# Two transformer-like blocks on one core: half of a projection tile moves behind the fourth branch's turns, a gate tile runs whole, and a copy goes ahead of an eviction

## The chip, the core and the metric

The kernel runs on one core of one Trainium2 chip. The core's engines run beside each other and meet only at semaphores: TensorE (PE in the profile; PEld is its weight load), VectorE (DVE), ScalarE (ACT), GpSimd (POOL) and SyncE (SP), which here only issues DMA. TensorE writes its products to PSUM, which has eight banks. The metric is the device time of one execution in microseconds, the median of the runs shown.

## The reference

All data are fp32, for 256 tokens of width 1024. A first block (attention and a linear recurrence, then a mixture of 16 experts) is followed by two layers of a second block. The change touches these two layers only. Cut to what matters, a layer is:

```
h = rmsnorm(x, norm_g[l])
c = split_columns(h @ w_in[l])                 # 1024 x 3564
y_a = attention A * silu(gate)                 # four branches, 4 heads of 64 each
y_b = attention B * silu(gate)
y_c = (compressed + selected + window) * silu(gate)
y_d = stick_breaking_attention(q, k, v) * silu(gate)
for i, y in enumerate((y_a, y_b, y_c, y_d)):
    gate = sigmoid(h @ w_merge[l, i] + b_merge[l, i])
    merged = merged + gate * (y @ w_branch[l, i])
x = x + merged @ w_out[l]
```

Stick-breaking attention, the fourth branch, takes for each query `a = exp(log_sigmoid(z) + after)`, where `after` sums `log_sigmoid(-z)` over the keys behind, and returns `a @ v`.

## The kernel before

A weight matrix is cut into tiles of 512 rows by 512 columns. SyncE loads a tile, ScalarE makes its high part (`high`, L426) and VectorE the rest (`low`, L435), each in two halves; every product then takes three matmuls, high by high, high by low and low by high. ScalarE's split of a tile waits until the tile before it in the ring of buffers is used.

In a layer, tiles 0 to 13 are the input projection `w_in` (L559, two tiles for one block of columns, 24 matmuls of 512 columns each; tiles 12 and 13 are block 6), and G[0] to G[15] are the gate products `h @ w_merge` (L639, 48 matmuls of 256 columns each). A block of products takes two PSUM banks, even blocks banks 0 and 1, odd blocks banks 2 and 3. The first gate block (G[0] and G[1]) has the banks of block 6, so its first matmul waits until ScalarE has evicted block 6 (`evict(6)`, L2611).

The attention runs in twelve groups: the kinds A, D, B, cmp, slc and win, each for the first and the second 128 query rows. Groups 2 and 3 are the fourth branch, D0 and D1 below. For a group TensorE makes the scores (L2504), VectorE and ScalarE turn them into probabilities (for D: ScalarE's L2735 to L2739, then VectorE's scans, then `exps` on ScalarE, L2747), TensorE turns these (L2574), ScalarE copies the turned ones from PSUM (`copies`, L2760), TensorE multiplies them by the values (L2584), and VectorE writes the output. A group with both halves of the keys does the turns and values in two rounds, D0 in one.

The order of each engine's work is written out by hand. TensorE's has two lists. `AHEAD[g]` is what it does between the scores and the wait for group g's exponentials; `BETWEEN[g][rd]` is what it does between the turns and the values of round rd. An entry `(i, k0, k1)` is part of tile i, in quarters: `(13, 0, 4)` is the whole of tile 13, `(G[0], 0, 2)` half of G[0]. In the loop (L2546 to L2587) the wait for the exponentials stands behind `AHEAD[g]` and ahead of the turns. The scores of both D0 and D1 are made before tile 12 is done. On ScalarE the order around the change is: `logs(3)` on D1's scores, `exps(2)` for D0, half a split (`feed(12, (1,))`, tile 15), `evict(6)`, `copies(2, 0)`, then `half_tanh(1)`, four squares (`squares`, L2660), `exps(3)`, a square root, `feed_gate(0)` (the split of tile 16, whose halves wait for the halves of G[0]) and `copies(3, 0)`. On GpSimd two copies of keys (L3238) wait for block 6's eviction.

Of the kernel before, what the change touches and what calls it, by code (L numbers as in the profile page):

```python
# [93 lines left out]
def two_blocks(nc, w, out, dbg=None):  # L94
# [3 lines left out]
    with ctx:  # L98
# [66 lines left out]
        def bank(b, n=1):  # L165
            return psum[:, b * 512:(b + n) * 512]
# [220 lines left out]
        def pair(g):  # L387
            return bank(2 * (g % 2), 2)
# [4 lines left out]
        def halves_of(n, r=0):  # L393

            return 2 * n + r * 2
# [19 lines left out]
        def high(act, i, r=0, parts=(0, 1)):  # L415

            n = tiles[i][1]
            if i == 0 and parts == (0,):
                act.wait_ge(first_half_in, 16)
            else:  # L420
                raw_landed(act, i, r)
            for part in parts:
                cols = slice(2 * n * part, 2 * n * part + 2 * n)
                if i >= SPLIT_SLOTS:
                    act.wait_ge(tile_used, halves_of(before_in_ring(i, r), r) + part + 1)
                nc.scalar.activation(hi_tile(i)[:, half_at(part, n)], raw_tile(i, n)[:, cols], ACT.Copy)\  # L426
                    .then_inc(hi_ready, 1)
# [1826 lines left out]
        def gate_tile(n):  # L2254

            return n + (W_GATE if n < GATES_FIRST else W_CMP + 2 - GATES_FIRST if n < GATES_LAST else
                        W_CMP + 4 - GATES_FIRST)
# [9 lines left out]
        def ahead(n):  # L2267

            return 3 if n + 3 < RING_TO or n >= RING_FROM - 2 else 4 if n in (W_CMP - 2, W_CMP - 1) else 2
# [7 lines left out]
        def turned_at(br, cc):  # L2277

            if br == 2:
# [11 lines left out]
        NR = FIRST_ROUND[NG]  # L2291

        G = [gate_tile(n) for n in range(16)]
        AHEAD = [[(5, 0, 4)], [(6, 2, 4)], [(13, 0, 4)], [(G[0], 2, 4)], [(G[5], 0, 4)], [(G[6], 2, 4)],
                 [("turn", 0, 1), (G[10], 0, 3)], [(G[11], 0, 2)], [("turn", 3), ("branch", 0, 0)], [("branch", 1, 0)],
                 [(G[12], 0, 2)], [(G[13], 0, 2)]]
        BETWEEN = [[(6, 0, 2)], [(7, 0, 2), (7, 2, 4)], [(G[0], 0, 2)], [(G[1], 0, 2), (G[1], 2, 4)],
                   [(G[6], 0, 2)], [(G[7], 0, 2), (G[7], 2, 4)], [(G[10], 3, 4)], [(G[11], 2, 4)],
                   [("branch", 0, 1)], [("branch", 1, 1, 0, 2), ("branch", 1, 1, 2, 4)],
                   [(G[12], 2, 4)], [(G[13], 2, 3), (G[13], 3, 4)]]  # L2300
# [63 lines left out]
        def layer_pe(pe, l):  # L2364
# [22 lines left out]
            def step(what, *parts):  # L2387
                if what == "turn":
                    turn_branches(*parts)
                elif what == "branch":  # L2390
                    branch_product(*parts)
                else:
                    filler(what, *parts)
# [152 lines left out]
            for g, (kind, t) in enumerate(GROUPS_L):  # L2546
# [10 lines left out]

                for part in AHEAD[g]:
                    step(*part)
# [6 lines left out]
                for rd in range(ROUNDS[g]):  # L2566
# [9 lines left out]
                    last.then_inc(l_turned, 1)  # L2576
                    step(*BETWEEN[g][rd])
                    pe.wait_ge(l_copied, m + 1 + l * NR)
# [18 lines left out]
        def layer_act(act, l):  # L2597
# [4 lines left out]
            def feed(n, parts=(0, 1)):  # L2602

                high(act, TB + n + ahead(n), r, parts)

            def evict(g):
                n = tiles[TB + 2 * g][1]
                j = COLUMN_BLOCKS[g]
                act.wait_ge(tile_used, halves_of(TB + 2 * g + 2, r))
                src = pair(BB + g).rearrange("p (t n) -> p t n", t=NT)[:, :, 0:n]  # L2610
                nc.scalar.activation(proj[:, :, 512 * j:512 * j + n], src, ACT.Copy)\  # L2611
                    .then_inc(block_free[(BB + g) % 2], 1)
# [128 lines left out]
            def exps(g):  # L2741
                kind, t = GROUPS_L[g]
                n = NCP if kind == "cmp" else (t + 1) * P
                p = probs[g % 2][:, :, 0:n]
                act.wait_ge(l_shift, g + 1 + l * NG)
                if kind == "D":
                    nc.scalar.activation(p, p, ACT.Exp).then_inc(l_exp, 1)  # L2747
                else:
                    for h in range(H2):
                        last = nc.scalar.activation(p[:, h, :], p[:, h, :], ACT.Exp, bias=l_nb[:, h:h + 1],  # L2750
                                                    accum_out=l_sum[:, h:h + 1])
                    last.then_inc(l_exp, 1)

            def copies(g, rd):
                m = FIRST_ROUND[g] + rd
                act.wait_ge(l_turned, m + 1 + l * NR)
                if m:
                    act.wait_ge(l_pv, m + l * NR)
                keys = NCP if GROUPS_L[g][0] == "cmp" else P
                nc.scalar.activation(pTs[0:keys, :], bank(6)[0:keys, :], ACT.Copy).then_inc(l_copied, 1)  # L2760
# [23 lines left out]
            logs(3)  # L2784
            exps(2)
            feed(12, (1,))
            evict(6)
            copies(2, 0)
            for g in (5, 6):
                evicted(g)  # L2790
            half_tanh(1, BG).then_inc(gates_ready, 1)
# [569 lines left out]
        @block.scalar  # L3361
        def _(act):
            first_act(act)
            moe_act(act)
            for l in range(LAYERS):
                own = layer_act(act, l)
                assert own.n == OWN_ACT, own.n
            last_act(act)
# [107 lines left out]
```

## Time and profile before

| | |
|---|---|
| runs | 1148.11, 1148.97, 1150.22 us; median 1148.97 |
| the profiled execution | 1150.05 us, its span 1148.3 us |
| TensorE busy, granted clock | 97% of the span, 0.997 of full |
| VectorE, ScalarE, GpSimd busy | 65%, 57%, 3% |
| DMA | 244 MB, 213 GB/s |
| first and second layer, the stretch of the change | about 690 to 716 us, and 955 to 981 us |

The table is to be read from TensorE's row: the other engines have room, but each has places where it is the one that TensorE waits for. Busy shares over the whole span do not show these; the timelines do.

### The profile page before, as it was taken

To read this page: it belongs to the slowest core of one execution; us is meant where nothing else is said; L and a number is where in the kernel's file an instruction comes from. 1 tells how busy PE (TensorE), PEld (TensorE's weight loads), DVE (VectorE), ACT (ScalarE), POOL (GpSimd) and SP (SyncE) were. 2 spreads that over 40 slices of the span, in tenths; PEclk is the share of its full clock that TensorE was granted. 3 is DMA by queue.
4 is the path that set the end of the run, shared out by engine and by line. 5 is a ranking of instruction groups with operands and counts; after the bars stand their busy time and mean duration, and the time that the engine had idled before them with its cause. 6 is when DMAs were issued, how large, how long until landed. Compare 5 with 4: busy or idle time off the path is not lost.

```text
span 1148.3 us, 18908 instructions
## 1 busy us (share of the span) xinstructions
PE 1116.2 (97%) x7741; PEld 967.6 (84%) x7741; DVE 742.1 (65%) x1064; ACT 659.3 (57%) x1097; POOL 38.4 (3%) x55
## 2 busy tenths in 40 slices
PE   8999999999999999998999999999999999999997
PEld 8887899998988887676876878899998887899995
DVE  5799948676999841312267647455887657455875
ACT  6487767744667842222246657556646558556652
POOL 1000000000001100000000000000000000000000
PEclk9999999999999999999999999999999999999999
DMA  9844452455579999999968543435546553436341
GB/s 340 309 147 146 137 195 85 137 183 173 175 278 304 354 376 379 387 387 387 387 238 315 162 167 111 146 108 188 180 149 209 181 178 116 145 113 220 112 148 55
DMA packets 118694, 244.19 MB, mean 213 GB/s; under 512 B 5281, under 2 KB 7489, under 8 KB 117712
## 3 DMA queue, kind: packets, MB, share of 16 engines
q1 hardware_dynamic: 113392, 228.96, 57.2%
q0 software_dynamic: 4160, 11.93, 2.9%
q10 hardware_dynamic: 1056, 2.10, 0.5%
q8 instruction: 61, 1.00, 0.3%
q14 instruction: 25, 0.20, 0.0%
HBM read 237.48 MB, written 9.44 MB: 215 GB/s over the span
## 4 chain that ended last, share of the span: by engine, by line
PE 77%; DVE 9%; DMA 5%; ACT 5%; issue 3%; SPq 1%; POOL 0%; DVEq 0%; POOLq 0%; ACTq 0%
PE psum L639 27%; PE psum L559 15%; PE psum L1405 4%; PE psum L574 4%; PE psum L2539 4%; PE psum L1415 3%; PE psum L1395 3%; PE psum L2584 3%; DVE weights_low L435 2%; DMA weights_raw<-in_w_in 2%; PE psum L1456 2%; ACT weights_high L426 1%; PE psum L2574 1%; PE psum L2504 1%; DMA arena<-in_w_expert_gate 1%
## 5 line engine op out<-in xcount | busy, mean ns | idle before, releaser
L435 DVE TENSOR_TENSOR weights_low<-weights_raw,weights_high 128x1024 fp32r<-128x1024 f32 x246 | 293.3, 1220 | 158.7 <-ACT weights_high L426 157.9
L426 ACT ACTIVATE weights_high<-weights_raw 128x1024 fp32r<-128x1024 f32 x246 | 254.6, 1056 | 147.8 <-PE psum L639 58.1
L639 PE MATMUL psum<-act_high,weights_high 128*128 128x256 f32 x896 | 258.0, 288 | 7.9 <-DVE weights_low L435 6.1
L639 PE MATMUL psum<-act_high,weights_low 128*128 128x256 f32 x896 | 249.7, 279 | 0.0
L639 PE MATMUL psum<-act_low,weights_high 128*128 128x256 f32 x896 | 249.6, 279 | 0.0
L639 PEld LDWEIGHTS psum<-act_high,weights_high 128*128 128x128 f32 x896 | 169.6, 189 | 15.6 <-issue 9.3
L639 PEld LDWEIGHTS psum<-act_high,weights_low 128*128 128x128 f32 x896 | 169.6, 189 | 0.6 <-issue 0.5
L639 PEld LDWEIGHTS psum<-act_low,weights_high 128*128 128x128 f32 x896 | 169.2, 189 | 0.0
L559 PE MATMUL psum<-weights_high,act_high 128*128 128x512 f32 (+1 forms) x256 | 102.4, 400 | 2.6 <-DVE weights_low L435 2.6
L559 PE MATMUL psum<-weights_high,act_low 128*128 128x512 f32 (+1 forms) x256 | 100.2, 391 | 0.0
L559 PE MATMUL psum<-weights_low,act_high 128*128 128x512 f32 (+1 forms) x256 | 100.1, 391 | 0.0
L559 PEld LDWEIGHTS psum<-weights_high,act_high 128*128 128x128 f32 x256 | 48.1, 188 | 15.7 <-DVE weights_low L435 3.8
L559 PEld LDWEIGHTS psum<-weights_high,act_low 128*128 128x128 f32 x256 | 48.1, 188 | 10.5
L559 PEld LDWEIGHTS psum<-weights_low,act_high 128*128 128x128 f32 x256 | 48.1, 188 | 9.7
L435 DVE TENSOR_TENSOR weights_low<-arena,weights_high 128x1024 fp32r<-128x1024 f32 x18 | 21.2, 1222 | 41.6 <-ACT weights_high L426 41.5
L2760 ACT ACTIVATE arena<-psum 128x512 f32<-128x512 f32 (+1 forms) x34 | 20.2, 595 | 47.4 <-PE psum L2574 47.4
L2750 ACT ACTIVATE arena<-arena,tiny 128x128 f32<-128x128 f32 (+2 forms) x80 | 33.0, 417 | 17.1 <-DVE tiny L3007 17.1
L426 ACT ACTIVATE xn_high<-weights_raw 128x1024 fp32r<-128x1024 f32 (+1 forms) x32 | 33.1, 1053 | 15.2 <-PE psum L559 6.2
L435 DVE TENSOR_TENSOR weights_low_third<-weights_raw,xn_high 128x1024 fp32r<-128x1024 f32 (+1 forms) x32 | 37.9, 1215 | 4.8 <-ACT xn_high L426 4.8
L453 ACT ACTIVATE arena<-x_tokens 128x1024 f32<-128x1024 f32 x10 | 10.6, 1062 | 38.5 <-DVE x_tokens L699 26.2
L639 PE MATMUL psum<-act_high,weights_low_third 128*128 128x256 f32 x112 | 31.3, 279 | 0.0
L2584 PE MATMUL psum<-arena 128*128 128x64 f32 x240 | 30.2, 268 | 1.0 <-ACT arena L2760 1.0
(503 smaller groups left out, 2354.1 us busy)
## 6 DMA issues: line engine op xcount, KB each, us to landing
weights_raw<-in_w_in SPq DMA_DIRECT2D x51, 1024.0 KB, 5.4
weights_raw<-in_w_merge SPq DMA_DIRECT2D x32, 1024.0 KB, 5.1
weights_raw<-in_w_expert_up SPq DMA_DIRECT2D x22, 1024.0 KB, 8.6
weights_raw<-in_w_expert_gate SPq DMA_DIRECT2D x17, 1024.0 KB, 8.6
arena<-in_w_expert_down SPq DMA_DIRECT2D x17, 1024.0 KB, 13.3
weights_raw<-in_w_expert_down SPq DMA_DIRECT2D x15, 1024.0 KB, 10.3
arena<-in_w_expert_gate SPq DMA_DIRECT2D x15, 1024.0 KB, 13.6
weights_raw<-in_w_out SPq DMA_DIRECT2D x12, 1024.0 KB, 5.1
```

The lines of the kernel that those rows point to most:

```text
L426: nc.scalar.activation(hi_tile(i)[:, half_at(part, n)], raw_tile(i, n)[:, cols], ACT.Copy)\
L435: dve.tensor_tensor(lo_tile(i)[:, half_at(part, n)], raw_tile(i, n)[:, cols], hi_tile(i)[:, half_at(part, n)].bitcast(f32), ALU.subtract). ...
L559: last = pe.matmul(pair(g)[:, t * 512:t * 512 + n], a[:, 4 * h + k, t * P:(t + 1) * P], b[:, chunk_at(k, n)], start=(h == 0 and k == 0 and ...
L574: return pe.matmul(pair(g)[:, t * 512:t * 512 + n], a[:, c0 + 4 * h + k, t * P:(t + 1) * P], b[:, chunk_at(k, n)], start=(h == 0 and k == ...
L639: last = pe.matmul(pair(g)[:, s * SEQ:(s + 1) * SEQ], b[:, k * 512 + s * P:k * 512 + (s + 1) * P], a[:, 4 * h + k, :], start=(h == 0 and k ...
L1395: last = pe.matmul(pair(g)[:, t * 512:(t + 1) * 512], a[:, c0 + k, t * P:(t + 1) * P], b[:, k * 512:(k + 1) * 512], start=(k == 0 and q == 0),
L1405: last = pe.matmul(out, a[:, k0 + k, cols], b[:, k * 512:(k + 1) * 512], start=(first and k == 0 and q == 0), stop=(final and k == 3 and q ...
L1415: last = pe.matmul(out[64 * h:64 * h + 64, :], stationary(k), raw_tile(i)[:, at:at + 256], start=(first and k == 0), stop=(final and k == ...
L1456: last = pe.matmul(small_out_bank(i)[64 * n:64 * n + 64, :], hidT_n[:, at:at + 64], raw_tile(tile)[:, 512 * k:512 * k + 512], start=(k == ...
L2539: last = pe.matmul(pair(g)[:, s * SEQ:(s + 1) * SEQ], b[:, at:at + P], a[:, 2 * br + kc, :], start=(kc == 0 and q == 0 and s % 2 == 0), st ...
L2584: last = pe.matmul(bank(7)[:, HD * h:HD * h + HD], pTs[0:keys, (hh * kts + kt) * P:(hh * kts + kt + 1) * P], values_of(kind, kt, h), start ...
L2750: last = nc.scalar.activation(p[:, h, :], p[:, h, :], ACT.Exp, bias=l_nb[:, h:h + 1], accum_out=l_sum[:, h:h + 1])
```

## The change

Three entries of TensorE's lists and two lines of ScalarE's order change. Before, TensorE ran the whole of tile 13 ahead of D0's turns, half of G[0] between D0's turns and values, and the other half of G[0] ahead of D1's turns. After, it runs half of tile 13 ahead of D0's turns, the other half between the turns and the values, and the whole of G[0] behind the values, ahead of D1's turns. ScalarE copies D0's turned probabilities before it evicts block 6, where it evicted first. Both layers run this code.

```diff
-        AHEAD = [[(5, 0, 4)], [(6, 2, 4)], [(13, 0, 4)], [(G[0], 2, 4)], [(G[5], 0, 4)], [(G[6], 2, 4)],
+        AHEAD = [[(5, 0, 4)], [(6, 2, 4)], [(13, 0, 2)], [(G[0], 0, 4)], [(G[5], 0, 4)], [(G[6], 2, 4)],
                  [("turn", 0, 1), (G[10], 0, 3)], [(G[11], 0, 2)], [("turn", 3), ("branch", 0, 0)], [("branch", 1, 0)],
                  [(G[12], 0, 2)], [(G[13], 0, 2)]]
-        BETWEEN = [[(6, 0, 2)], [(7, 0, 2), (7, 2, 4)], [(G[0], 0, 2)], [(G[1], 0, 2), (G[1], 2, 4)],
+        BETWEEN = [[(6, 0, 2)], [(7, 0, 2), (7, 2, 4)], [(13, 2, 4)], [(G[1], 0, 2), (G[1], 2, 4)],
@@ ScalarE @@
             logs(3)
             exps(2)
             feed(12, (1,))
+            copies(2, 0)
             evict(6)
-            copies(2, 0)
             for g in (5, 6):
                 evicted(g)
```

## Rows read from the trace of the kernel before

**Rows 1.** The page: busy us of each engine; the chain that ended last, by engine.
```profile
PE 1116.2 (97%) x7741; PEld 967.6 (84%) x7741; DVE 742.1 (65%) x1064; ACT 659.3 (57%) x1097; POOL 38.4 (3%) x55
PE 77%; DVE 9%; DMA 5%; ACT 5%; issue 3%; SPq 1%; POOL 0%; DVEq 0%; POOLq 0%; ACTq 0%
```
**Rows 2.** TensorE's waits: who waited for whom, us in total, times, longest us.
```profile
PE psum L639 <- DVE weights_low L435: 6.1, 6, 3.4
...
PE psum L639 <- ACT arena L2611: 1.6, 2, 0.8
...
PE psum L574 <- DVE weights_low_third L435: 1.0, 1, 1.0
PE psum L2584 <- ACT arena L2760: 1.0, 2, 0.5
```
**Rows 3.** Timeline of TensorE: start us, us, engine, line, operation, tiles, count, idle before.
```profile
692.94 0.39 PE L559 MATMUL psum<-xn_high,act_high 128*128 128x512 f32 x1
...
698.43 0.60 PE L2574 MATMUL psum<-params,arena 128*128 128x128 f32 x4
699.82 0.39 PE L639 MATMUL psum<-act_high,weights_high 128*128 128x256 f32 x1 [0.79 <-ACT arena L2611]
...
702.65 1.00 PE L2584 MATMUL psum<-arena 128*128 128x64 f32 x8
703.46 0.36 PE L639 MATMUL psum<-act_high,weights_high 128*128 128x256 f32 x1
...
706.25 0.28 PE L639 MATMUL psum<-act_low,weights_high 128*128 128x256 f32 x1
706.60 0.66 PE L2574 MATMUL psum<-params,arena 128*128 128x128 f32 x4
707.01 0.36 PE L639 MATMUL psum<-act_high,weights_high 128*128 128x256 f32 x1
...
710.50 1.10 PE L2584 MATMUL psum<-arena 128*128 128x64 f32 x8 [0.49 <-ACT arena L2760]
711.44 0.61 PE L2574 MATMUL psum<-params,arena 128*128 128x128 f32 x4
711.80 0.37 PE L639 MATMUL psum<-act_high,weights_high 128*128 128x256 f32 x1
...
965.57 0.39 PE L639 MATMUL psum<-act_high,weights_high 128*128 128x256 f32 x1 [0.79 <-ACT arena L2611]
```
**Rows 4.** Timeline of ScalarE through the same stretch.
```profile
690.19 1.03 ACT L2735 ACTIVATE arena<-psum 128x1024 f32<-128x1024 f32 x1 [0.29 <-PE psum L2504]
...
697.27 0.63 ACT L2747 ACTIVATE arena<-arena 128x512 f32<-128x512 f32 x1
697.81 1.05 ACT L426 ACTIVATE weights_high<-weights_raw 128x1024 fp32r<-128x1024 f32 x1
698.76 1.00 ACT L2611 ACTIVATE arena<-psum 128x1024 f32<-128x1024 f32 x1
...
705.49 1.06 ACT L2747 ACTIVATE arena<-arena 128x1024 f32<-128x1024 f32 x1 [3.01 <-DVE arena L2990]
...
707.97 2.00 ACT L426 ACTIVATE weights_high<-weights_raw 128x1024 fp32r<-128x1024 f32 x2
709.88 0.57 ACT L2760 ACTIVATE arena<-psum 128x512 f32<-128x512 f32 x1
712.08 0.60 ACT L2760 ACTIVATE arena<-psum 128x512 f32<-128x512 f32 x1 [1.64 <-PE psum L2574]
```
**Rows 5.** Stage windows: us, busy of each engine (count), granted clock, DMA share, GB/s.
```profile
544.00:548.00 4.00, 3.95 (x20) 3.98 (x21) 3.73 (x4) 2.01 (x2) 0.00 (x0) 0.57 1.05 387
...
612.00:616.00 4.00, 3.24 (x18) 2.59 (x19) 3.96 (x6) 1.98 (x4) 0.00 (x0) 1.00 1.05 356
716.00:903.00 187.00, 186.50 (x1419) 169.89 (x1418) 125.76 (x191) 111.72 (x215) 3.48 (x6) 1.00 0.50 167
```
**Rows 6.** Timeline of GpSimd in the stretch.
```profile
699.95 1.17 POOL L3238 COPY arena<-arena 128x256 f32<-128x256 f32 x2 [89.29 <-ACT arena L2611]
```

## The prediction

> **What bounds the kernel now.** I began with the page's busy line and the chain that ended last: TensorE is busy for 1116.2 of 1148.3 us and holds 77% of the chain [rows 1]. So an edit pays only where TensorE stands still, and it costs where it makes TensorE stand still. TensorE's waits come next [rows 2]. Two kinds lie in the stretch that the diff touches, once in each layer: the first gate tile's matmuls (L639) behind an eviction (L2611), 0.8 us, and the value products (L2584) behind a copy (L2760), 0.5 us. The other two rows there, 3.4 and 1.0 us, are from other stages and are used below for the clock. Then TensorE's timeline through the stretch, where each wait can be placed and priced [rows 3], and ScalarE's beside it, to see what each wait hangs on [rows 4]. A stage window closes it: from 716 to 903 us TensorE is busy for 186.50 of 187 us [rows 5]. After the stretch there is no slack in which a delay could be lost: whatever shift it ends with reaches the end of the span.
>
> Durations on TensorE need care: ends are modelled and overlap the next start, so I count from start to start. One matmul of a 512-wide tile costs 0.229 us that way (692.94 to 698.43 for the 24 of tile 13).
>
> **The stretch before, piece by piece** (layer 0, from tile 13's first matmul at 692.94) [rows 3]: tile 13, 5.49; the four turns of D0 (the fourth branch's first rows) at 698.43, some 0.35 of work (the turns at 711.44, which waited for nothing, take 0.36 to their successor); a stall to 699.82, 1.04; half of G[0], 2.83; D0's values, 0.81; the other half of G[0], 703.46 to 706.37 (its last start, 706.25, and one step more), 2.91; a stall of 0.23 to the turns of D1 at 706.60; these turns, 0.41; half of G[1], 2.83 as the other that followed a stop, to 709.84; a stall of 0.66 to D1's first values at 710.50; these, 0.94. They end at 711.44: 18.5 us in all.
>
> The three stalls hang on ScalarE [rows 4]. The first is the eviction of block 6: it starts at 698.76, when tile 13 is used and the split at 697.81 is out of the way, and ends at 699.76; G[0] needs its PSUM banks. The second is the exponential of D1, 705.49 + 1.06 = 706.55. The third is the copy of D1's first turns, 709.88 + 0.57 = 710.45, behind both halves of tile 16's split at 707.97.
>
> **What the change moves.** TensorE's order becomes: tile 13's first half, turns D0, its second half, values D0, G[0] whole, turns D1. No matmul is added or removed, no DMA is moved. ScalarE takes the copy ahead of the eviction.
>
> *Added, first:* the turns need the exponential of D0 (L2747 at 697.27, ending 697.90). Before, the whole of tile 13 lay over it, and TensorE came to the turns 0.5 us after it was done. Now it comes after 12 matmuls, at 692.94 + 12 x 0.229 = 695.68. Nothing in the change makes the exponential earlier: ahead of it on ScalarE stands the work on D1's scores, from 690.19 on and without a gap, and those scores were made before tile 13. TensorE starts 0.05 after such an end (706.55 to 706.60), so at 697.95: **2.27 us of new stall**. Queued behind the turns on TensorE are the rest of tile 13, so the eviction, and G[0]. The turns take 0.41, as after the other stall: to 698.36. Tile 13's second half takes 12 x 0.229 and 0.08 for the stop before it (the first matmul after turns lasts 0.36, at 707.01, where the others last 0.28): 2.82, to 701.18. The copy for D0 now follows the split that ends at 698.86, so it is done by 699.4 and costs the values no wait: 0.81, to 701.99.
>
> *Added, second:* the eviction waits for tile 13, whose last matmul starts at 700.95 and ends 0.39 later. ScalarE, when free, begins 0.03 after such an end (turns 711.44 + 0.61, copy 712.08). So 701.37 to 702.37, G[0] at 702.43 (0.06 later, as 699.76 to 699.82). The values cover 0.81 of it, and **0.44 us of stall is left**. Bounds: nothing, if the values cover it all; 1.04, as before, if they cover nothing.
>
> *Removed:* the old 1.04. G[0] runs in one piece: 2.83 + 2.91 less 0.09 for the stop between, 5.65, to 708.08. The turns of D1 come long after 706.55: the 0.23 is gone and they take 0.36, to 708.44. Half of G[1], 2.83, to 711.27. Is the copy of 710.45 still on time? It stands behind tile 16's split, whose second half needs G[0] used, some 708.3, and would not start before 708.9 anyway. Yes: the 0.66 is gone, and the values take 0.81 in place of 0.94, to **712.08**.
>
> The sum for one layer: +2.27 +0.06 +0.08 +0.44 added; -1.04 -0.23 -0.66 for the stalls and -0.09 -0.05 -0.13 for the stops; +0.65. So 712.08 against 711.44, **+0.65 us a layer**. Layer 1 has the same two waits [rows 2] and the same stretch 265.75 us later (G[0] at 965.57 [rows 3]), so +1.3 us in all.
>
> **What covers the moved ScalarE work.** From the eviction's start to the end of the squares it is 3.7 us before (698.76 to 702.48, which is 705.49 less the idle 3.01), less some 0.5 for the copy, which is now ahead. They end near 704.6, still before 705.49, when VectorE releases D1's exponential. If that cover failed, the exponential has 1.5 us in hand before TensorE asks for it at 708.08. GpSimd's two key copies, 1.17 us, follow the eviction too [rows 6]; they move to 702.6, beside VectorE's steps for D1. I take nothing for that: all 1.17 us on that chain would stay inside the 1.5. SyncE's loads wait for splits, not for tile 13's products, and keep their order.
>
> **A rule weighed.** After TensorE's longest wait, 3.4 us [rows 2], the granted clock was 0.57 of full from 544 to 548 us, between the levels of 1.2 and 2.4 GHz. After the wait of 1.0 us in layer 0's first tile it stayed at 1.00 [rows 5]. The Trainium skill, "TensorE: Matmul & The Clock Gate", section "HAM oscillation — how this bites in real kernels", speaks against this change: idle gaps in TensorE's work send its clock to the lower level, and the matmuls after them pay for it. By that rule the new gap would cost more than its length, as in rival B.
>
> **The rivals.**
>
> A, **the exchange is even** (1149.0). It takes 0.65 us a layer: a shorter road to D0's exponential, or a later wait that takes up the shift. For it: only that the difference is small beside the 2.9 us added. Against it: no gap in rows 4 ahead of the exponential, and a full TensorE after it [rows 5]. 8%.
>
> B, **the new gap drops the clock** (slower). 2.27 us, with short turns behind it, lies between the 1.0 that did nothing and the 3.4 that did. That wait cost 4 us at 0.57, so 1.7 us. Once a layer: 1.3 + 3.4 = 4.7, 1153.7 us. It decides only from the gap at which the clock falls, and this gap is a third shorter than the one that is known to do it. 8%, and 3% for a fall in one layer only (1152.0).
>
> C, **the next wait stays** because something else is late: D1's copy behind the split that waits for G[0], or D1's exponential behind key copies and squares. The price is the 0.66 and 0.23 a layer at most: 1.3 + 1.8 = 3.1, 1152.1. It decides if G[0] is used more than 0.6 us later than worked out. 6%.
>
> D, **the change brings its gain** (faster). If the turns did not wait, the 2.27 and 0.06 would be gone and each layer 1.7 us shorter: 1145.6. It needs the exponential by 695.7; it ends at 697.90. 2%.
>
> **How the numbers follow.** The forecast, 73%, is +1.3 us. The profiled execution took 1150.05 us (1148.3 of span), so it would take 1151.35; the median of the runs shown is 1148.97, and on that scale it is **1150.3 us**. The range: the eviction's stall from 0 to 1.04 a layer gives +0.4 to +2.5 us; the even exchange is 1149.0, the fall in one layer 1152.0; with the spread of the runs, 1148.11 to 1150.22, I take 1148.7 to 1152.4. A measurement of this kernel can tell about 0.2%, 2.3 us. Slower than 1151.3: B, half of C and some 8 of the main case's 73, 0.22. Faster than 1146.7: D and one of the main case, 0.03. The rest, 0.75, is within.
>
> **What would show it.** In the changed trace: turns D0 some 2.3 us after tile 13's twelfth matmul, their idle time ended by L2747; no wait of L639 right behind the turns, but one of 0.3 to 0.5 us behind the values; D1's turns and first values without a wait; D0's copy some 2 us before the eviction; from there to the layer's end the old timeline, 0.65 us later. The prediction is wrong if the turns wait for under 1.5 us, if the clock around 696 to 704 is under 1.00, or if the wait before D1's first values is still there.

## The result

| | median | runs |
|---|---|---|
| before | 1150.22 us | 1148.11 to 1152.14, 9 runs |
| changed | 1154.07 us | 1152.14 to 1156.66, 9 runs |

The ratio is 1.0033, with a 95% interval of 1.0022 to 1.0044: the change makes the kernel 3.85 us slower at the median, where +1.3 us was forecast. Measured once more on another occasion it was 1.0024 (1.0015 to 1.0034). The median of before is also 1.25 us over that of the first three runs, on which the forecast stood; that part of the distance between 1150.3 and 1154.07 says nothing of the change.

The profiled execution of the changed kernel took 1152.58 us, its span 1150.8. TensorE's waits in it (who waited for whom, us in total, times, longest us) answer to [rows 2]:

```profile
PE psum L639 <- DVE weights_low L435: 5.8, 6, 3.3
PE psum L2574 <- ACT arena L2747: 4.2, 2, 2.1
...
PE psum L639 <- ACT arena L2611: 0.5, 2, 0.3
```

The second row is new: in each layer the turns of D0 wait 2.1 us for the exponential. The wait for the eviction went from 0.8 to 0.3 us, and the wait of the values (L2584) for the copy, the last of [rows 2], is no longer listed at all. TensorE's timeline through the stretch in layer 0, which answers to [rows 3]:

```profile
692.00 0.39 PE L559 MATMUL psum<-xn_high,act_high 128*128 128x512 f32 x1
...
697.00 0.66 PE L2574 MATMUL psum<-params,arena 128*128 128x128 f32 x4 [2.09 <-ACT arena L2747]
...
700.26 1.00 PE L2584 MATMUL psum<-arena 128*128 128x64 f32 x8
701.53 0.39 PE L639 MATMUL psum<-act_high,weights_high 128*128 128x256 f32 x1 [0.27 <-ACT arena L2611]
...
707.30 0.60 PE L2574 MATMUL psum<-params,arena 128*128 128x128 f32 x4
...
710.47 1.00 PE L2584 MATMUL psum<-arena 128*128 128x64 f32 x8
711.31 0.61 PE L2574 MATMUL psum<-params,arena 128*128 128x128 f32 x4
```

Counted from tile 13's first matmul, with the forecast in brackets: the turns of D0 at 5.00 us (5.01), its values at 8.26 (8.24), G[0] at 9.53 (9.49), the turns of D1 at 15.30 (15.14), the next turns at 19.31 (19.14; before, 18.50). The step by step working holds to 0.2 us. And in layer 1 the same stretch, 959.43 to 978.57, is 19.14. So this execution holds +0.81 and +0.64, 1.45 us of own length, where 1.3 was forecast. Its span is 2.5 us over before's; the other 1.05 us lie outside the stretch (see "Still open"), and what the runs have beyond 2.5 us is not in this profile. ScalarE's rows show the rest as forecast, the copy well ahead of the eviction (compare [rows 4]):

```profile
696.32 0.63 ACT L2747 ACTIVATE arena<-arena 128x512 f32<-128x512 f32 x1
696.85 1.04 ACT L426 ACTIVATE weights_high<-weights_raw 128x1024 fp32r<-128x1024 f32 x1
697.80 0.58 ACT L2760 ACTIVATE arena<-psum 128x512 f32<-128x512 f32 x1
700.46 1.02 ACT L2611 ACTIVATE arena<-psum 128x1024 f32<-128x1024 f32 x1 [2.08 <-PE psum L559]
...
704.16 1.06 ACT L2747 ACTIVATE arena<-arena 128x1024 f32<-128x1024 f32 x1 [0.25 <-DVE arena L2990]
```

What gave the cause away was another column. Every run comes with TensorE's mean granted clock. The clocks of before's nine runs are not on record, so the later occasions must give them. The nine of the changed kernel have 0.992 to 0.997, and time goes with it: 1152.14 us at 0.996, 1154.07 at 0.994, 1156.66 at 0.992. The profiled one was the best, at 0.997. So theory 1 is rival B, the new gap drops the clock in some executions; theory 2 is that the gap costs its own length only.

### The profile page after: what moved, and what is told of

Its sections match the earlier page's. It is cut to its first block, busy times and chain, and to the rows that moved or that the text cites. A ratio compares the mean times of both kernels' runs of the same rounds, so it can differ in the third digit from the quotient of the medians.

```text
span 1150.8 us, 18908 instructions
## 1 busy us (share of the span) xinstructions
PE 1117.6 (97%) x7741; PEld 969.9 (84%) x7741; DVE 741.6 (64%) x1064; ACT 659.7 (57%) x1097; POOL 37.5 (3%) x55
## 4 chain that ended last, share of the span: by engine, by line
PE 78%; DVE 9%; ACT 5%; DMA 4%; issue 3%; SPq 0%; POOL 0%; DVEq 0%; POOLq 0%; ACTq 0%
PE psum L639 28%; PE psum L559 16%; PE psum L1405 4%; PE psum L574 4%; PE psum L2539 4%; PE psum L1415 3%; PE psum L2584 2%; DVE weights_low L435 2%; PE psum L1395 2%; PE psum L1456 2%; PE psum L2574 2%; PE psum L2504 1%; DMA arena<-in_w_expert_gate 1%; DMA weights_raw<-in_w_expert_gate 1%; ACT weights_high L426 1%
## 5 line engine op out<-in xcount | busy, mean ns | idle before, releaser
L2760 ACT ACTIVATE arena<-psum 128x512 f32<-128x512 f32 (+1 forms) x34 | 20.2, 594 | 50.0 <-PE psum L2574 50.0
L2584 PEld LDWEIGHTS psum<-arena 128*128 128x128 f32 x240 | 29.8, 191 | 0.6
```

Source lines behind the costliest of these rows:

```text
L2584: last = pe.matmul(bank(7)[:, HD * h:HD * h + HD], pTs[0:keys, (hh * kts + kt) * P:(hh * kts + kt + 1) * P], values_of(kind, kt, h), start ...
```

## The experiments

**The changed kernel again, with every run's clock beside before's.**

> The changed kernel once more, beside the kernel before, to read the granted clock of every run. Its profiled span was 2.5 us over that of before, of which the two stretches hold 0.8 and 0.65 us, but the runs were 3.8 us slower at the median. Theory 1 (the new gap drops TensorE's clock in some executions): its runs have a mean granted clock that scatters below 0.997, while those of before stay near 0.997, and the time goes with it: 1.7 us for each stretch at half clock, which is 0.0015 of the mean. Theory 2 (the gap costs only its own length, and the rest is the pace that differs between executions): both kernels' runs have the same scatter of the clock, and the difference is 1.4 us, ratio 1.0012.

Measured: ratio 1.0024 (1.0015 to 1.0034); its 12 runs have a mean clock of 0.9956, the 23 of before beside them 0.9967. Taken over all occasions, the clock is 0.995 or less in 13 of 22 runs of the changed kernel (mean 0.9950) and in 12 of 76 of before (mean 0.9964). The runs of the changed kernel at 0.996 and more have a mean of 1152.2 us, those of before 1150.0: +2.2 us with most of the clock loss left out, +3.2 us over all. Theory 1 stands so far. That clean difference is nearer to 2 than to 1.4, which neither theory expected.

**One more profile of the changed kernel**, to see where the clock falls.

> One more profile of the changed kernel, to find an execution whose clock fell outside the experts' stage. Theory 1: where the mean clock is 0.995 or less, the clock's record has a stretch of 3.4 us at half level that begins at or just behind the gap near 695 or 962 us. Theory 2: such stretches, if any, lie elsewhere.

Its mean clock was 0.994, its time 1153.61 us. Windows of the new profile (us, busy of PE, PEld, DVE, ACT, POOL with counts, granted clock, DMA share, GB/s), first of the changed kernel's first profile, then of this one:

```profile
694.00:698.00 4.00, 1.91 (x11) 1.30 (x11) 2.91 (x4) 3.97 (x5) 0.00 (x0) 1.00 0.00 0
698.00:702.00 4.00, 3.73 (x23) 3.17 (x21) 3.97 (x6) 1.83 (x3) 0.34 (x1) 1.00 0.36 106
```

```profile
694.00:698.00 4.00, 1.89 (x9) 1.24 (x8) 3.18 (x4) 3.96 (x5) 0.00 (x0) 1.00 0.01 3
698.00:702.00 4.00, 4.00 (x13) 3.20 (x14) 3.69 (x6) 1.27 (x2) 0.00 (x0) 0.57 0.11 38
```

In both, TensorE is busy for half of the first window. In the second profile, its clock then falls (0.57 over 4 us, so 1.2 GHz for 3.4 of them) and 13 matmuls start where 23 did. The timeline of the same execution shows it begin just behind the gap:

```profile
697.89 0.66 PE L2574 MATMUL psum<-params,arena 128*128 128x128 f32 x4 [2.11 <-ACT arena L2747]
698.30 0.59 PE L559 MATMUL psum<-xn_high,act_high 128*128 128x512 f32 x1
698.69 0.63 PE L559 MATMUL psum<-weights_low_third,act_high 128*128 128x512 f32 x1
699.12 0.63 PE L559 MATMUL psum<-xn_high,act_low 128*128 128x512 f32 x1
```

The matmuls of tile 13's second half start 0.43 us apart, where they are 0.23 apart at 2.4 GHz. From tile 12's second half to D1's second turns this layer took 23.59 us against 22.20 in its layer 1, with the same gap and no fall: **a fall costs 1.4 us**. The gap is 2.11 us in both layers, so the gap makes the fall possible, not certain.

Two cautions. This execution's mean clock of 0.994 is not the gap's alone: its clock fell in three places before TensorE's work ended, and the other two (0.62 from 544 to 548 us, in the experts, and 0.72 from 608 to 612 us, in layer 0's first tile) are places where before's clock falls too. And the mean takes in the tail of the span, where TensorE has no matmul left and a fall costs nothing (0.85 from 1142 to 1146 us in before's first profile). So a single mean does not say where the clock fell; only the difference between the kernels does.

**Matmuls in the gap.** Identity products into a free PSUM bank, placed in `layer_pe` ahead of the wait; they add work and change no result.

```diff
+                if g == 2:
+                    pe.wait_ge(l_copied, FIRST_ROUND[g] + l * NR)
+                    keep_warm(pe, 6, ident, 18)
                 pe.wait_ge(l_exp, g + 1 + l * NG)
```

> The changed kernel with 18 matmuls of the identity into a PSUM bank that is free, in place of standing still ahead of the turns of D0 (some 2.0 of the 2.1 us idle); nothing of the result depends on them. Theory 1 (clock): the mean granted clock stays at 0.997 in every run, and the time is 1.3 to 1.6 us over before, ratio 1.0012, some 2 us below the changed kernel. Theory 2 (own length only): the same time as the changed kernel, clock and all.

Measured: ratio 1.0051 (1.0037 to 1.0065), clock 0.9968. The dose was wrong: the filling itself is the row

```profile
694.51 4.18 PE L711 MATMUL psum<-params 128*128 128x128 f32 x36
```

36 matmuls for 18, since each fp32 product goes through twice, and 4.18 us in a gap of 2.1. So the time says nothing against the changed kernel's; only the clock, 0.995 once and 0.997 or more in the other four runs, does. With 8 in place of 18:

> As the fill before, but with 8 matmuls of the identity: the 18 took 4.18 us (each goes through TensorE twice, 0.116 us a pass) and overran the gap by some 2 us; 8 take 1.86 us of the 2.1 us gap. Theory 1 (the gap drops the clock in some executions): mean granted clock as of before (0.9967), time 1.3 to 2.3 us over before, ratio 1.0011 to 1.0020, and under the changed kernel's 1.0024 to 1.0033. Theory 2 (no clock loss from the gap): ratio and clock as the changed kernel's.

Measured: ratio 1.0015 (1.0006 to 1.0025), clock 0.9965, beside before's 0.9965. Its gap lies from 696.4 to 698.7 us; the windows, to set beside those above:

```profile
694.00:698.00 4.00, 4.00 (x26) 3.55 (x25) 3.18 (x6) 3.95 (x4) 0.00 (x0) 1.00 0.17 67
698.00:702.00 4.00, 3.67 (x21) 2.97 (x20) 3.66 (x6) 2.09 (x4) 0.00 (x0) 1.00 0.05 4
```

The turns start no earlier and no later, G[0] and the rest follow as in the changed kernel (22.20 us from tile 12's second half to D1's second turns in both layers, against 21.37 before), and the clock loss is gone. This separates the two shares: the length alone is 1.0015, the changed kernel is 1.0024 and 1.0033. Theory 2 falls. The intervals of 1.0015 and 1.0024 touch, so the size of the clock's share rests on the clock column more than on this pair of times.

**A shorter gap.** Three quarters of tile 13 ahead of the turns: `(13, 0, 3)` in `AHEAD[2]`, `(13, 3, 4)` in `BETWEEN[2]`.

> The changed kernel with three quarters of tile 13 ahead of the turns of D0 and one quarter behind. Both theories: the turns come at 692.94 + 18 x 0.229 = 697.06 on the old time scale and wait 0.9 in place of 2.3 us; behind the values of D0 0.3 to 0.5 us of waiting for the eviction; G[0] ends near 706.7, the turns of D1 do not wait, their first values wait 0.2 to 0.6 us for the copy. A layer is 0.1 to 0.4 us shorter than before: ratio 0.9993 to 1.0000. Theory 1: no clock loss, since the gap is under the 1.0 us that did nothing: clock 0.997 throughout.

Measured: ratio 0.9998 (0.9989 to 1.0006), clock 0.9965. The wait is 0.7 us, and the stretch is 21.17 us in place of 21.37, 0.2 us less in each layer. No clock loss at this length. Its gain is too small for the runs to tell from none.

**A longer gap.** One quarter ahead: `(13, 0, 1)` and `(13, 1, 4)`.

> The changed kernel with one quarter of tile 13 ahead of the turns of D0 and three behind: TensorE stands still for 2.1 + 1.4 = 3.5 us ahead of the turns. Own length: 1.4 us a layer more than the changed kernel, so 2.2 a layer over before, 4.4 us. Clock: if a longer gap makes the fall surer, as the two executions seen with a fall in the stretch suggest, it comes in nearly every execution and in both layers: two stretches of 3.41 us at half level, mean granted clock 0.9935 or less (before 0.9966, less 0.003), and 3.4 us more: ratio 1.0060 to 1.0075. If the clock does not hang on the gap's length, the clock is as the changed kernel's (0.995) and the ratio 1.0045 to 1.0055.

Measured: ratio 1.0063 (1.0045 to 1.0081), clock 0.9925, under the bound given. Both layers fall in its profile:

```profile
PE psum L2574 <- ACT arena L2747: 7.0, 2, 3.5
```

```profile
698.00:702.00 4.00, 3.96 (x14) 3.20 (x15) 3.69 (x6) 1.42 (x2) 0.00 (x0) 0.64 0.15 23
...
968.00:972.00 4.00, 3.67 (x12) 2.99 (x13) 3.69 (x5) 1.71 (x3) 0.00 (x0) 0.60 0.16 19
```

The stretch takes 25.14 and 24.95 us: 1.4 more than the changed kernel's 22.20 for the longer gap, and 1.4 to 1.6 for the fall. The gap's length goes with how sure the fall is: at 0.7 us the clock is before's (0.9965), at 2.1 it is 0.9950, at 3.5 it is 0.9925. The Trainium skill, "TensorE: Matmul & The Clock Gate", section "HAM oscillation — how this bites in real kernels", has idle gaps send the clock to its lower level and the work after them pay; at 3.5 us the trace agrees, with the rows above. The section warns of gaps longer than 2.1 us, and here the measurement goes further than it: the changed kernel's 2.11 us was enough in some executions.

**The two parts of the change alone.** First TensorE's lists as changed with ScalarE's old order:

```diff
+            evict(6)
             copies(2, 0)
-            evict(6)
```

> TensorE's lists as changed, ScalarE's order as before: the eviction of block 6, then the copy of D0. The eviction waits for tile 13, so the copy and the values of D0 stand behind it: values at some 1.0 us later than in the changed kernel, G[0] 1.3 us later, nothing after that to take it up. A layer is 1.3 us longer than in the changed kernel, 2.6 us in all: ratio to before 1.0045 to 1.0055.

Measured: ratio 1.0086 (1.0071 to 1.0102), well over the expectation. The length was right where the clock held: layer 1's stretch took 23.40 us, 1.2 more than the changed kernel's. But the mean clock was 0.9913, the lowest of all, and layer 0 took 26.56 us. Its waits and windows show why:

```profile
PE psum L2574 <- ACT arena L2747: 4.2, 2, 2.1
PE psum L2584 <- ACT arena L2760: 3.2, 2, 1.6
```

```profile
697.00:701.00 4.00, 3.84 (x13) 3.12 (x14) 3.69 (x6) 1.06 (x2) 0.00 (x0) 0.60 0.15 21
701.00:705.00 4.00, 2.40 (x14) 1.85 (x13) 3.11 (x4) 2.77 (x7) 1.48 (x2) 0.93 0.64 241
705.00:709.00 4.00, 4.00 (x24) 4.00 (x24) 1.36 (x4) 3.30 (x8) 0.00 (x0) 0.61 0.01 4
```

A second gap of 1.6 us stands behind the first, and the clock falls twice. So the order on ScalarE belongs to the move: without it the moved half tile costs 0.86%, some three times the changed kernel's 0.24 to 0.33%.

Then the kernel before with only the copy ahead of the eviction:

> TensorE's lists as before, only the copy of D0 ahead of the eviction on ScalarE. The eviction then waits for the turns of D0 and the copy: it starts 0.8 us later, G[0] starts at 700.6 instead of 699.8. The shift is taken up by the 0.23 us ahead of the turns of D1 and the 0.66 us ahead of their first values, which wait for a copy that hangs on ScalarE: net 0.0 to 0.1 us a layer, ratio 1.0000 to 1.0002. If the copy's time went through, it would be 1.6 us, 1.0014.

Measured: ratio 1.0003 (0.9993 to 1.0012), clock 0.9972, nothing that can be told from no change. TensorE's rows:

```profile
700.90 0.39 PE L639 MATMUL psum<-act_high,weights_high 128*128 128x256 f32 x1 [1.60 <-ACT arena L2611]
...
711.66 0.61 PE L2574 MATMUL psum<-params,arena 128*128 128x128 f32 x4
```

The wait for the eviction doubles, from 0.79 to 1.60 us, yet the stretch is 0.05 us shorter than before's (21.31 us in both layers): what came late was taken up by the waits that follow. It also shows what a stall in this place was worth: nothing, since TensorE waits for ScalarE again two steps on. And 1.60 us of idle time, with short turns ahead of it, brought no fall in either layer and no lower mean clock: one more length on the scale.

**Where the clock fell, over all profiles.** Thirteen executions were profiled, each with two passes of the stretch. Where TensorE stands idle in it for 2.1 us or more (the changed kernel three times, one quarter, and the lists with the old ScalarE order), the clock fell in 4 of 10 passes; with no more than 1.6 us, or with the gap filled, in none of 16. For the changed kernel alone it is 1 pass of 6.

**What the place has to give.** If the last of these waits is what sets the stretch, it should be attacked by itself. It hangs on ScalarE's order: the copy of D1's turns behind both halves of tile 16's split.

```diff
-            feed_gate(0)
-            copies(3, 0)
+            feed(gate_tile(0), (0,))
+            copies(3, 0)
+            feed(gate_tile(0), (1,))
```

First on top of the version with three quarters:

> The version with three quarters ahead, and on ScalarE the copy of D1's first turns between the two halves of tile 16's split instead of behind both. The three-quarter version still waited 0.24 us for that copy and then 0.1 us for the restart. If ScalarE's order is what it waits for, both go: 0.5 us a layer under before, 1.1 us in all, ratio 0.9988 to 0.9993, clock as before's. If the wait moves to the next copy (which hangs on TensorE's own turns) the ratio stays at 0.9997.

Measured: ratio 0.9984 (0.9974 to 0.9993), clock 0.9972, a little more gain than expected; the stretch 20.82 us, 0.55 less than before in each layer, where 0.5 was expected. What the runs have beyond 1.1 us the stretch does not show. Then the same edit alone, on the kernel before:

> The kernel before with one change: ScalarE copies D1's first turns between the two halves of tile 16's split. TensorE's order is untouched, with the whole of tile 13 over D0's exponential. In the kernel before, D1's first values waited 0.66 us for that copy and took 0.13 more for the restart. If the gain of the version with three quarters came from this copy, and not from the moved tile, both go here too: the stretch from tile 12's second half to the next turns takes 20.6 us in place of 21.4, 0.8 us a layer, 1.6 us in all, ratio 0.9984 to 0.9990, clock as before's. If the moved tile is what pays, the ratio stays at 0.9996 or above.

Measured: 1147.76 us against 1149.75, ratio 0.9986 (0.9977 to 0.9995), and the stretch 20.60 us in both layers, as expected. In the rows of ScalarE and TensorE the copy (L2760) now ends before TensorE has done half of G[1], and the values follow it with no wait:

```profile
706.19 1.04 ACT L426 ACTIVATE weights_high<-weights_raw 128x1024 fp32r<-128x1024 f32 x1
707.14 0.58 ACT L2760 ACTIVATE arena<-psum 128x512 f32<-128x512 f32 x1
707.62 1.05 ACT L426 ACTIVATE weights_high<-weights_raw 128x1024 fp32r<-128x1024 f32 x1
```

```profile
704.82 0.66 PE L2574 MATMUL psum<-params,arena 128*128 128x128 f32 x4
708.05 1.00 PE L2584 MATMUL psum<-arena 128*128 128x64 f32 x8
708.89 0.61 PE L2574 MATMUL psum<-params,arena 128*128 128x128 f32 x4
```

So the gain was the copy's, not the moved tile's; on top of it the moved quarter costs 0.22 us a layer by the stretch, which the runs (0.9984 and 0.9986) can't tell. This version, with the tile lists as they were before, is faster than the kernel before, and so than the changed one.

**The kernel before, profiled once more.**

> The kernel before, profiled once more, to see which of its stretches keep their length from one execution to the next. Theory 1: the stretch of the change is 21.4 us in both layers to a few hundredths, and what differs is the matmuls' pace elsewhere (0.113 or 0.118 us a gate matmul) and falls of the clock in the experts or at the first layer's start. Theory 2: the stretch itself scatters by some tenths, so that the 0.8 us of the changed kernel is partly chance.

Measured: 1149.41 us, span 1147.6. The stretch is 21.36 us in both layers, the first profile's to a hundredth. It had a fall of the clock from some 608.5 us on, in layer 0's first tile, and none in the experts, where the first profile had its one [rows 5]; both have one more in the tail, where it costs nothing. Before's clock scatters too, then, but it does so elsewhere. The wait ahead of that fall, and the windows of the experts and of the tile:

```profile
608.38 0.65 PE L574 MATMUL psum<-weights_high,act_high 128*128 128x512 f32 x1 [0.91 <-DVE weights_low L435]
544.00:548.00 4.00, 3.44 (x30) 3.47 (x31) 4.00 (x5) 2.59 (x5) 0.00 (x0) 1.00 1.05 387
608.00:612.00 4.00, 3.62 (x9) 2.68 (x10) 4.00 (x11) 3.97 (x7) 1.56 (x3) 0.57 1.05 384
```

So the clock fell behind 0.91 us of idle time, with another 0.90 us two microseconds earlier, in a place where the first profile kept it through the same two waits and one of 1.05 us. And it held at 1.00 behind 2.79 us in the experts, where 2.77 us dropped it in the changed kernel's third profile.

## Why the prediction was wrong

**The arithmetic of the stretch was right.** The new stall was 2.09 to 2.11 us idle (2.27 from start to start), the turns at the forecast instant to 0.01 us; what is left of the eviction's wait is 0.3 us idle; the three old stalls went as the working said; nothing later took the shift up. 1.45 us in the first profile, and 0.82 to 0.85 in the three layers without a fall of its other two profiles, so some 1.66 for two, against 1.3. The mis-sized term is G[0]: I gave it 5.65 us, and it took 5.77 in layer 0 and 5.56 in layer 1 of the same execution (701.53 to 707.30, 968.99 to 974.55), by the pace at which its matmuls start, 0.118 or 0.1135 us.

**The step that failed is the weighing of rival B.** The mechanism was named, its price set at 1.7 us a fall (1.4 measured in the stretch), and it was given 8% and 3%, because the gap was "a third shorter than the one that is known to do it" and lay above 1.0 us, "that did nothing". Two rows of one profile were read as a yes and a no, and neither holds for every execution: behind waits of 0.90 and 0.91 us, in the very tile whose 1.0 us did nothing, the clock of before fell in its second profile, and 2.79 us did nothing in the experts. The section of the Trainium skill that the prediction names was no better guide to this gap: it warns of gaps longer than 2.1 us. The runs show a fall that comes in some executions: the same 2.11 us gap dropped the clock in one layer and not in the next. With an outcome like that, what matters is not whether it happens in the likeliest execution but how much it adds to the median.

By the clock column: 0.9964 less 0.9943 in the first nine runs, and one fall of 3.4 us at half clock is 0.0015, so 1.4 falls an execution, some 2 to 2.4 us. With 1.45 of length that is 3.4 to 3.9, beside 3.85 measured. In the later runs (0.9956, beside before's 0.9967) it is some 0.7 falls, 1.0 to 1.2 us, 2.5 to 2.7 in all, beside a ratio of 1.0024, 2.8 us. These are estimates, and they close too well: runs with a good clock are 2.2 us over, not 1.45, so by the times the clock's share is nearer 1.6 us in the first nine runs and 0.6 in the later ones. That the share is there is shown; its size is known only to a factor of two or so. Of the distance between 1150.3 and 1154.07, 1.25 us is the scale on which the forecast stood.

**The other rivals.** A did not happen: [rows 5]'s full TensorE behind the stretch held (186.51 of 187 us in the same window). C did not happen: the split of tile 16 and the squares were in time, as worked out. D did not happen. What I took for nothing and shouldn't have: the key copies on GpSimd. Before, they ran beside VectorE's four scans for D1, which took 2.79 us; in the changed kernel they come later and the scans take 2.43 (2.58 with three quarters of the tile ahead, 2.74 with only the copy moved). The rows, before's first and the changed kernel's third profile:

```profile
700.03 2.79 DVE L2983 TENSOR_TENSOR_SCAN arena<-arena 128x256 f32<-128x256 f32 x4
699.96 2.43 DVE L2983 TENSOR_TENSOR_SCAN arena<-arena 128x256 f32<-128x256 f32 x4
```

It was a gain of 0.36 us on the chain to D1's exponential, with 1.5 us in hand, so it moved nothing.

**Still open:** runs of the changed kernel with a good clock are 2.2 us over before's, the stretch holds 1.5 to 1.7. Part of the rest shows in the profiles as matmul pace outside the stretch: from the start of layer 0's last turns to the stretch of layer 1 the changed kernel's first two profiles take 128.93 and 128.92 us, before's two 128.40, and from the start of layer 1's last turns to TensorE's last matmul 47.85 against 47.18. But the changed kernel's third profile has 128.36 and 47.21, and the three-quarter version with the split, the second fastest, has 128.93 and 47.85. So the pace is not the change's own. It may come more often with it: the long form, 1.2 us in all, is in 5 of the 9 profiles with part of tile 13 behind the turns (in both places each time) and in none of the 4 with the whole tile ahead. At that rate it would be worth the missing 0.6 us, but 13 profiles can't tell this from chance, and no run tested it.

## What to carry to other kernels

Before a block of work is moved from ahead of a wait to behind it, ask what it was covering there: tile 13 looked like mere work, and it hid the last 2.3 us of the chain to an exponential. A new gap on TensorE is priced by its length plus the chance of a clock fall behind it; that chance shows in the mean clock over many runs and can be absent from any one profile. A wait that kept the clock in one execution is no proof that it will in the next. And of several waits in a row, look for the one that the later steps hang on: doubling the first here cost nothing, while removing the last gave 0.14%.

## What the runs showed of the hardware

- A fall of TensorE's clock is not decided by the program alone: with a gap of 2.1 us it came in one layer and not the other. The mean clock over the runs was 0.9965 with 0.7 us and 0.9972 with 1.6 (before: 0.9964), 0.9950 with 2.1, 0.9925 with 3.5, 0.9913 with 2.1 and 1.6 close together, and 0.9965 with the 2.1 filled by matmuls. Nor is it decided by the length of one wait: it fell behind two of 0.9 us (608 us, before's second profile) and held behind 2.79 us (544 us, the same profile).
- Matmuls of one kind start at one of two paces for long stretches at the same granted clock of 1.00: 0.1135 or 0.118 us for the gate matmuls, 0.229 or 0.233 us for the 512-wide ones (48 of them from 853 us on: 0.229 in before's first profile, 0.233 in the changed kernel's). Which one holds changes at stops, and differs from one execution to the next.
- VectorE's scans took 2.79 us for the four while GpSimd's copies read beside them, and 2.43 us without.
